# A decoder layer on one core: the gate tables of PEER computed between the weight tiles of peer_u, from one-hots that keep tokens innermost

## The reference

```python
def peer_ffn(x, w_q, sub_keys, u_tab, v_tab):
    ...
    qry = (xt @ w_q).reshape(N, PEER_HEADS, 2, PEER_DKEY // 2).astype(jnp.float32)
    s = jnp.einsum('nhpd,pkd->nhpk', qry, sub_keys.astype(jnp.float32))
    s_top, i_top = lax.top_k(s, K)
    cand = (s_top[:, :, 0, :, None] + s_top[:, :, 1, None, :]).reshape(N, PEER_HEADS, K * K)
    cand_id = (i_top[:, :, 0, :, None] * PEER_NKEYS + i_top[:, :, 1, None, :]).reshape(N, PEER_HEADS, K * K)
    best, pos = lax.top_k(cand, K)
    expert = jnp.take_along_axis(cand_id, pos, axis=-1)
    gate = jax.nn.softmax(best, axis=-1)
    ...
        u = u_tab[ec]
        hid = jax.nn.gelu(jnp.einsum('cd,chkd->chk', xc, u).astype(jnp.float32), approximate=False)
        w = (gc * hid).astype(x.dtype)
        return jnp.einsum('chk,chkd->cd', w, v_tab[ec])
```

## Time and profile before

| | us |
|---|---|
| median of three runs | 1181.72 |
| the profiled execution | 1181.99 |
| its span, first to last instruction | 1180.2 |
| PE busy | 1101.1 (93%) |
| DVE busy | 812.0 (69%) |
| ACT busy | 619.8 (53%) |
| POOL busy | 547.8 (46%) |

### The profile page before, as it was taken

The page is one execution under the profiler, slowest core; times in us unless marked ns, Lnnn a source line. Parts: engine busy times, 40 slices in busy tenths (PEclk is TensorE's granted clock), DMA queues, the critical chain, the costliest instruction groups (busy, mean ns, idle before and its releaser), DMA issues.

```text
span 1180.2 us, 21974 instructions
## 1 busy us (share of the span) xinstructions
PE 1101.1 (93%) x6734; PEld 972.6 (82%) x6734; DVE 812.0 (69%) x1329; ACT 619.8 (53%) x882; POOL 547.8 (46%) x419
## 2 busy tenths in 40 slices
PE   6999999978999999999999976668999999999995
PEld 5888887668999999999999975557888888888884
DVE  4448654564467777777777799996666666666666
ACT  4357544542345555555545568996444444545452
POOL 5474345443443333433333336554555555555554
PEclk9999999997999999999999998999999999999998
DMA  6654443342455555555555540003555555555552
GB/s 223 219 195 143 143 161 125 125 143 89 161 172 184 178 180 185 185 178 180 187 184 178 180 141 1 0 0 121 182 193 182 193 181 192 185 188 185 188 189 95
DMA packets 52456, 186.34 MB, mean 158 GB/s; under 512 B 6208, under 2 KB 6592, under 8 KB 52432
## 3 DMA queue, kind: packets, MB, share of 16 engines
q1 hardware_dynamic: 51584, 182.87, 44.9%
q0 software_dynamic: 848, 3.15, 0.8%
HBM read 184.94 MB, written 1.05 MB: 158 GB/s over the span
## 4 chain that ended last, share of the span: by engine, by line
PE 80%; DVE 7%; issue 6%; ACT 3%; DMA 2%; POOL 1%; DVEq 1%; SPq 0%; ACTq 0%; POOLq 0%
PE ps L1173 16%; PE ps L1175 15%; PE ps L1174 15%; PE ps L1464 10%; PE ps L1465 10%; PE ps L1466 10%; DVE raw_ij L1066 2%; PE ps L1213 1%; DMA raw<-w_tiles_in 1%; ACT whi L471 1%; DVE wlo L728 1%; POOL wlo L323 1%; ACT hot_j L673 1%; PE ps L1400 1%; DVE xt L944 1%
## 5 line engine op out<-in xcount | busy, mean ns | idle before, releaser
L323 POOL TENSOR_TENSOR wlo<-raw,whi 128x256 fp32r<-128x256 f32 x341 | 446.6, 1310 | 567.5 <-ACT whi L471 566.7
L471 ACT ACTIVATE whi<-raw 128x1024 fp32r<-128x1024 f32 x344 | 364.3, 1059 | 472.0 <-DMA raw<-w_tiles_v 177.3
L728 DVE TENSOR_TENSOR wlo<-raw,whi 128x768 fp32r<-128x768 f32 x341 | 337.1, 989 | 274.8 <-ACT whi L471 256.9
L1173 PE MATMUL ps<-ahi,whi 128*128 128x256 f32 x1152 | 328.9, 285 | 2.6 <-DVE alo L975 1.4
L1175 PE MATMUL ps<-ahi,wlo 128*128 128x256 f32 x1152 | 327.3, 284 | 0.0
L1174 PE MATMUL ps<-alo,whi 128*128 128x256 f32 x1152 | 327.2, 284 | 0.0
L1173 PEld LDWEIGHTS ps<-ahi,whi 128*128 128x128 f32 x1152 | 222.5, 193 | 3.2 <-DVE alo L975 1.8
L1174 PEld LDWEIGHTS ps<-alo,whi 128*128 128x128 f32 x1152 | 222.5, 193 | 0.0
L1175 PEld LDWEIGHTS ps<-ahi,wlo 128*128 128x128 f32 x1152 | 222.3, 193 | 0.0
L1464 PE MATMUL ps<-whi,hhi 128*128 128x512 f32 x512 | 202.5, 395 | 1.1 <-POOL wlo L323 1.1
L1465 PE MATMUL ps<-wlo,hhi 128*128 128x512 f32 x512 | 202.2, 395 | 0.0
(11 more groups left out here) (193 smaller groups left out, 1014.9 us busy)
## 6 DMA issues: line engine op xcount, KB each, us to landing
raw<-w_tiles_u SPq DMA_DIRECT2D x128, 512.0 KB, 3.2
raw<-w_tiles_v SPq DMA_DIRECT2D x128, 512.0 KB, 3.2
raw<-w_tiles_in SPq DMA_DIRECT2D x64, 512.0 KB, 3.3
raw<-w_tiles_q SPq DMA_DIRECT2D x16, 512.0 KB, 3.3
raw<-w_tiles_out SPq DMA_DIRECT2D x8, 512.0 KB, 3.2
xraw<-xT SPq DMA_DIRECT2D x4, 256.0 KB, 6.1
xt<-x POOLq DMA_DIRECT2D x1, 1024.0 KB, 5.3
out<-xt SPq DMA_DIRECT2D x4, 256.0 KB, 2.1
```

The source lines that it names most:

```text
L323: pool.tensor_tensor(wlo[:, tile.slot, DVE_COLS:], raw[:, tile.slot, DVE_COLS:], whi[:, tile.slot, DVE_COLS:].bitcast(F32), ALU.subtract)\
L471: act.activation(whi[:, tile.slot, :], raw[:, tile.slot, :], ACT.Copy)\
L728: dve.tensor_tensor(wlo[:, tile.slot, 0:DVE_COLS], raw[:, tile.slot, 0:DVE_COLS], whi[:, tile.slot, 0:DVE_COLS].bitcast(F32), ALU.subtract)\
L1173: pe.matmul(out, ah, bh, start=start, stop=False)
```

## The change

Tables are made in chunks of 4 tokens instead of blocks of 8, and not after peer_u but between its tiles: 32 chunks after every second tile from tile 29 on, 32 after every tile from tile 92 on (`after`). For this, the routing of the first token tile is done beside the queries and the first 21 tiles of peer_u, that of the second beside tiles 21 to 79, for all heads in a row; the lookup of expert numbers comes once per token tile, in operations of 1024 bf16 elements. The choices are transposed after tiles 23 and 83.

`hot_i` and `hot_j` keep the tokens innermost, as `raw_ij` has them, so ACT and POOL read and write contiguously, and TensorE reads both operands of a token's table with a step of four fp32. ACT widens all of i, POOL scales all of j.

A chunk meets an H of which only the first `there` = after(c) + 1 rows exist. DVE multiplies those by the table and copies the table into the rows to come. GELU of a later tile goes, for tokens whose table is already there (`late_tokens`), to `gelu_late`, and DVE multiplies it into H (`merge`); for the others straight to H. All PEER loops on DVE, ACT and POOL in this stage are written out instead of looped.

```diff
+BLK = 4
...
+RING = (0, 1)
+SEL_BANKS = (6, 7)
+VB = (0, 1, 6, 7)
...
+ONE_PER_TWO, ONE_PER_TILE = 28, 92
+SEL_AT = (23, 83)
+EXP_AT = (20, 79)
...
+def after(c):
+
+    if c < HALF_CHUNKS:
+        return ONE_PER_TWO + 2 * c + 1
+    return ONE_PER_TILE + c - HALF_CHUNKS
...
+def routing_steps(t, u):
+
+    if t == 0:
+        return 2 - u % 2
+    return int(u % 8 != 7)
...
+    hot_i = place("hot_i", [P, HOTS, P, BLK])
+    hot_j = place("hot_j", [P, HOTS, P, BLK])
...
+        def scale_j(c):
+
+            pool.wait_ge(S["hot_ready"], c + 1)
+            if c >= HOTS:
+                pool.wait_ge(S["g_done"], c + 1 - HOTS)
+            pool.tensor_tensor(hot_j[:, c % HOTS, :, :], raw_ij[:, c % HOTS, 1, :, :],
+                               gateT[:, None, c * BLK:(c + 1) * BLK].to_broadcast([P, P, BLK]), ALU.mult)\
+                .then_inc(S["hot_j_ready"], 1)
...
+        def widen_i(c):
+
+            act.wait_ge(S["hot_ready"], c + 1)
+            if c >= HOTS:
+                act.wait_ge(S["g_done"], c + 1 - HOTS)
+            act.activation(hot_i[:, c % HOTS, :, :], raw_ij[:, c % HOTS, 0, :, :], ACT.Copy)\
+                .then_inc(S["hot_i_ready"], 1)
...
+        for u in range(TILES_U):
+            if u == 96:
+                act.wait_ge(S["sel_tp"], NT)
+            late = late_tokens(u)
+            act.wait_ge(S["tiles_used"], T_U + u + 1)
+            if late > 0:
+                if u - FIRST_LATE >= NTMP:
+                    act.wait_ge(S["merged"], u - FIRST_LATE - NTMP + 1)
+                last = act.activation(gelu_late[:, u % NTMP, 0:late], ps[:, HID[u % 4], 0:late], ACT.Gelu)
+            if late < SEQ:
+                last = act.activation(H[:, u, late:SEQ], ps[:, HID[u % 4], late:SEQ], ACT.Gelu)
+            last.then_inc(S["hid_used"], 1)
+            c = CHUNK_AFTER.get(u + 1)
+            if c is not None:
+                widen_i(c)
+            split_hi(Tile(T_U + u + AHEAD))
...
+        def into_h(c):
+
+            there = after(c) + 1
+            dve.wait_ge(S["g_done"], c + 1)
+            dve.wait_ge(S["hid_used"], there)
+            toks = slice(c * BLK, (c + 1) * BLK)
+            g = ps[:, RING[c % 2], :].rearrange("p (n i) -> p i n", i=NK)
+            dve.tensor_copy(H[:, there:NK, toks], g[:, there:NK, :])
+            dve.tensor_tensor(H[:, 0:there, toks], H[:, 0:there, toks], g[:, 0:there, :], ALU.mult)\
+                .then_inc(S["g_used"], 1)
...
+        for u in range(TILES_U):
+            if u >= FIRST_LATE:
+                merge(u)
+            c = CHUNK_AFTER.get(u)
+            if c is not None:
+                into_h(c)
...
+            c = CHUNK_AFTER.get(u + 2)
+            if c is not None:
+                hots(c)
+            split_lo(Tile(T_U + u + AHEAD))
...
+            for _ in range(routing_steps(int(u > EXP_AT[0]), u)):
+                next(steps, None)
...
+            if u >= H_DONE:
+                split_h(Tile(T_V + u - H_DONE))
...
+            for k in range(BLK):
+                last = pe.matmul(ps[:, RING[b], k * P:(k + 1) * P], hot_j[:, b, :, k], hot_i[:, b, :, k],
+                                 start=True, stop=True)
+            last.then_inc(S["g_done"], 1)
...
+        hidden(SEL_AT[1] + 1, ONE_PER_TILE, 2, (SEL_AT[1] + 1 - ONE_PER_TWO) // 2)
+        hidden(ONE_PER_TILE, after(CHUNKS - 1) + 1, 4, HALF_CHUNKS)
+        hidden(after(CHUNKS - 1) + 1, TILES_U)
...
+        pe.wait_ge(S["g_used"], CHUNKS)
+        pe.wait_ge(S["selT_done"], NT)
```

More of the change, by code:

```diff
@@ L981, in _ @@
         x1_low(1)
[L984 to L992, removed]
@@ L1038, in _ @@
-        spare_hold(dve, S["sc_copied"], TILES_Q)
[L1039 to L1045, removed]
-                if k == 7:
-                    for _ in steps:
-                        pass
-            own.leave(NT * PH - 1)
-        def by_head(a):
-            return a.rearrange("p (u k) -> p u k", k=TOPK)
@@ new lines, in merge @@
+        def merge(u):
+            late = late_tokens(u)
+            dve.wait_ge(S["hid_used"], u + 1)
+            dve.wait_ge(S["g_used"], late // BLK)
+            dve.tensor_tensor(H[:, u, 0:late], H[:, u, 0:late], gelu_late[:, u % NTMP, 0:late], ALU.mult)\
+                .then_inc(S["merged"], 1)
+        steps = routing(0)
+        for k in range(TILES_Q):
+            split_lo(Tile(T_Q + k + AHEAD))
+            dve.wait_ge(S["sc_done"], k + 1)
+            dve.tensor_copy(sc[:, k, :, :], ps[:, k % 2, 0:2 * NK].rearrange("p (t k) -> p t k", t=NT))\
+                .then_inc(S["sc_copied"], 1)
+            if k >= 2:
+                for _ in range(routing_steps(0, k)):
+                    next(steps, None)
@@ L1147, in split_h @@
                 .then_inc(S["w_lo"], 1)
+        for u in range(TILES_U):
+            if u >= FIRST_LATE:
[3 more added lines that the diff above has]
+                into_h(c)
+            for t in range(NT):
+                if u == SEL_AT[t] + 1:
+                    take_sel(t)
+            c = CHUNK_AFTER.get(u + 2)
+            if c is not None:
+                hots(c)
+            split_lo(Tile(T_U + u + AHEAD))
+            if u in EXP_AT:
+                assert next(steps, True)
+            if u == EXP_AT[0] + 1:
+                steps = routing(1)
+            for _ in range(routing_steps(int(u > EXP_AT[0]), u)):
+                next(steps, None)
+            for t in range(NT):
+                if u == EXP_AT[t] + 1:
+                    gates(t)
+            if u >= H_DONE:
+                split_h(Tile(T_V + u - H_DONE))
         for k in range(4):
@@ L1415, in _, with hidden @@
+        def hidden(first, end, chunks=0, base=0):
+            with pe.Fori(first // 4, end // 4) as i:
+                for k in range(4):
+                    pe.wait_ge(S["hid_used"], i * 4 + (k - 3))
+                    by_tokens(Tile(T_U + k, i, 4), HID[k])
+                    if chunks == 4 or chunks == 2 and k % 2 == 1:
+                        n = k if chunks == 4 else k // 2
+                        gate_tables(n % 2, (chunks, base + n - first // 4 * chunks), i)
         for k in range(1, 4):
@@ L1434, in gate_tables @@
-        def gate_tables(n, b, i=None):
-            if i is None:
-                pe.wait_ge(S["hots_wide"], n + 1)
-                pe.wait_ge(S["j_scaled"], n + 1)
-            else:
-                pe.wait_ge(S["hots_wide"], i * GB + (b + 1))
-                pe.wait_ge(S["j_scaled"], i * GB + (b + 1))
-                pe.wait_ge(S["g_used"], i * GB + (b + 1 - GB))
-            for k in range(BLK):
-                last = pe.matmul(ps[:, 2 * b + k // 4, (k % 4) * P:(k % 4 + 1) * P], hot_j[b % HOTS][:, k, :],
-                                 hot_i[b % HOTS][:, k, :], start=True, stop=True)
-            last.then_inc(S["g_done"], 1)
```

365 lines of the change are left out of this document (152 added, 213 removed).

## The result

The changed kernel takes 1199.99 us at the median (1197.57 to 1200.62, 4 runs) against 1181.88 for the kernel before (now four runs): a ratio of 1.0149, interval 1.0131 to 1.0167. It is slower by 18 us, and the interval leaves out 1. The prediction said 1144 and faster.

A forecast was written before the change was run, and what follows sets the result against it. TensorE was taken to bound peer_u and peer_v, VectorE the stage between. 1181.99 - 108.7 + 59.5 = 1132.8, plus 3 and 6 for VectorE and 2 for chunk starts and ends: 1144 us; own range 1131 to 1160, with rivals 1130 to 1198.

The forecast's parts named there:

- The middle stage goes: Between peer_u and peer_v: TensorE's weight work stands still for 108.7 us, all removed, with nothing back at the seam.
- 256 tables at the contiguous price: Between peer_u's weight tiles: 64 chunks of 8 table records at 0.93 us each add 59.5 us.
- The stride at 0: TensorE's table operands at a step of four fp32: taken to cost nothing extra, bounded above by +59.5 us, further out +210.
- The rule cited from the Trainium skill: Table operand reads: 16-byte lines need two hits for full speed, so one hit pays an unsized penalty; spoke against the change.
- VectorE, +9 us: VectorE's work moved beside query and peer_u tiles: 3 us and 6 us of it come to the path.
- R2: Rival: TensorE's strided read runs at half speed in every table, slower than before, 1195 us; chance 0.25.
- part (a): Query tiles 2 to 15 and peer_u tiles 0 to 20: VectorE 113 us against TensorE's 106.5, 3 on the path.
- part (b): Peer_u tiles 28 to 79, 26 pairs: VectorE 6.9 us a pair against TensorE's 6.66, 6 us to the path.
- (c): Peer_u tiles 92 to 125: VectorE 3.45 us a tile against TensorE's 3.79, nothing on the path.
- R1: Rival: VectorE becomes the bound, through its load and GpSimd's blocking; 1165 us half-way up the bounds, 1190 all the way; chance 0.18.
- R3: Rival: each table record streams its operand twice at ACT's 2.06 ns an element, 0.53 us a record, 1346 us; chance 0.04.
- R4: Rival: each chunk stalls TensorE by the latency of one-hots, widening, tables and H, up to about 1 us; 1175; chance 0.07.

## Why the prediction was wrong

*The middle stage goes, 108.7 us.* Right: the matmuls at the seam are 0.12 us apart, so nothing came back there.

*256 tables at the contiguous price, 59.5 us.* Right for contiguous operands: 0.89 us a chunk, where 0.93 was taken, so 57 us in all.

*The stride at 0.* This is the step that failed. The prediction bounded it from 0 to +59.5 us (and +210 far out) and chose 0, because "if a value is read once for both, TensorE needs a value only every 0.92 ns there, half of what it takes elsewhere". The condition holds: the one-pass tables show that a record reads each value once. The conclusion did not follow. A fetch from 16 bytes of its own takes 1.84 ns, twice the 0.92 at which values are needed, and a record grew from 0.112 to 0.235 us. The 0.92 should have been compared with the one row that priced such a fetch, ACT's 2.06 ns; that row was used for upper bounds only, and 128 x 2.06 = 0.26 us a record stood within reach of the 0.235 measured. The term put at 0 measured 64 x 1.08 = 69 us by the chunks, 64.5 by the medians.

*The rule cited from the Trainium skill* ("Advanced Engine Details and Errata", section "SBUF Cachelines") was the better guide: pieces of 16 bytes, full speed with two hits on each. TensorE's records agree: 0.118 us at a step of two, near the 0.112 contiguous, then 0.176 at three and 0.235 at four.

*VectorE, +9 us.* In the changed kernel beside the slow tables it is hidden, as R2 had it; the 2.1 us of waits for `wlo` all fall in part (a). With contiguous tables 6.2 us of waits show: part (a) was put at 3 and measured 2.2, part (b) at 6 and measured 4.0. The sizes inside: the one-hots, taken at 0.9, had a mean of 0.697 in the changed kernel and of 0.850 with contiguous tables (0.686 at the median, 1.256 at the longest), and GpSimd's `hot_j` was longer, 1.09 at its fastest and 1.69 beside DVE's splits, where 1.26 was taken. Two slips did no harm: nine steps at 1.6 are 14.4 us in (a), not 16, and the chunks of (c) follow 32 tiles, 92 to 123, not 34. The bound of 1.0 us a pair in (b) stands without its working. R1, which had VectorE as the bound at 1165, did not come about.

*Rivals.* R2 is what happened, with a chance of 0.25, and its sign, records about 0.24 us apart and no waits, is what the trace shows. It said 1195. The chunk measured 1.97 us where R2 has 0.93 + 0.93 = 1.86, which is 7 us more in all, and the 3 us that R2 adds for VectorE do not show in the total. The range ended at 1198, 2 us short of the time. R3 (each value fetched twice) needs 0.53 us a record and 1346, and is excluded by the 0.235; R4 (each chunk stalls) by the windows, which are full.

## What to carry to other kernels

Moving VectorE's work on the tables into the shadow of the weight tiles paid 46 us here, 1181.5 to 1135.5, although TensorE still has 57 us of tables to do; the layout that came with it took 64.5 back. So price a layout by the engine that bounds the stage it moves to: ACT and GpSimd, idle for about half of the time, did the turning for 0.05 and 0.02 us more a chunk, while TensorE paid 1.08 for not having it done. And where an unseen price has a row on another engine, compare it with the slack in nanoseconds per value before calling it hidden.

## What the hardware showed that I had not expected

When both operands are strided, TensorE's time for a record of 128 values follows the 16-byte pieces that it touches, 1.83 to 1.88 ns each, once that exceeds the 0.112 us of contiguous operands: 0.118 us at a step of two fp32, 0.176 at three, 0.235 at four, 0.240 at eight. The streamed operand and the weight load have nearly the same price, and they overlap: at step four one strided operand costs 0.227 (stream) or 0.233 us (weights), both 0.235. Of one operand alone only step four was tried. A one-pass record at step four takes 0.234, the same as one of two passes, and contiguous it takes 0.112 us, again the same, and not half of the 0.12 that 256 columns take.
